# Hybrid encoder block on one core: norm weights spread by GpSimd, gate columns packed, setup reordered on three engines

## What is computed

```python
def rmsnorm(x, w):
    y = x * lax.rsqrt(jnp.mean(x * x, axis=-1, keepdims=True) + EPS)
    return y * w

h = rmsnorm(x, norm_w)
proj = h @ w_in          # 1024 x 6168: DeltaNet q, k, v, z and the 8-wide beta and alpha,
                         # attention q, k, v, z and the 8-wide forget logits, two merge gates
y_a = gated_deltanet(...)            # chunks of 64 tokens, 8 heads
y_b = forgetting_attention(...)      # softmax with a decay from the forget logits
x = x + (g_a * (y_a @ P_A) + g_b * (y_b @ P_B)) @ W_out
out = rmsnorm(x, final_norm_w)
```

## Time and profile before

| | |
|---|---|
| median of 3 runs | 949.03 us (947.95 to 949.48) |
| span of the profiled execution | 945.6 us |
| TensorE busy | 925.3 us (98%) |
| VectorE, ScalarE, GpSimd busy | 65%, 50%, 2% |
| DMA, mean | 111 GB/s |

### The profile page before, as it was taken

The page is one execution under the profiler, slowest core; times in us unless marked ns, Lnnn a source line. Parts: engine busy times, 40 slices in busy tenths (PEclk is TensorE's granted clock), DMA queues, the critical chain, the costliest instruction groups (busy, mean ns, idle before and its releaser), DMA issues.

```text
span 945.6 us, 15912 instructions
## 1 busy us (share of the span) xinstructions
PE 925.3 (98%) x6380; PEld 700.9 (74%) x6380; DVE 610.6 (65%) x982; ACT 471.8 (50%) x842; POOL 19.7 (2%) x28
## 2 busy tenths in 40 slices
PE   5999999999999999999999999999999999999997
PEld 4778787888888876676766666666667888888885
DVE  7487568799999934454496786767862433246252
ACT  7555654532866625532756547556554442334131
POOL 1000002020000000000000000000000000000000
PEclk9999999999999999999999999999999999999999
DMA  8111351249323393322553325234125323123162
GB/s 251 45 49 45 96 178 48 68 143 228 100 90 104 107 271 89 102 74 91 139 181 94 109 101 168 102 102 123 35 68 178 108 71 94 51 112 112 45 192 75
DMA packets 115744, 104.87 MB, mean 111 GB/s; under 512 B 34192, under 2 KB 95760, under 8 KB 115288
## 3 DMA queue, kind: packets, MB, share of 16 engines
q1 hardware_dynamic: 104008, 80.27, 30.6%
q10 hardware_dynamic: 10512, 19.40, 5.6%
q0 software_dynamic: 1152, 4.19, 1.3%
HBM read 76.84 MB, written 27.00 MB: 110 GB/s over the span
## 4 chain that ended last, share of the span: by engine, by line
PE 45%; DVE 3%; ACT 1%; DMA 1%; issue 1%; SPq 0%; DVEq 0%; ACTq 0%
PE pj L2182 6%; PE pj L2184 5%; PE pj L2183 5%; PE pc L2315 4%; PE pa L2281 3%; PE pa L2250 1%; PE pj L2193 1%; PE pj L2195 1%; PE pj L2194 1%; PE pb L2341 1%; PE pb L2330 1%; PE pc L2450 1%; PE pc L2449 1%; PE pb L2450 1%; PE pb L2449 1%; PE pa L2450 1%
## 5 line engine op out<-in xcount | busy, mean ns | idle before, releaser
L144 PE MATMUL pj<-h_hi,w_hi 128*128 128x512 f32 x504 | 203.6, 404 | 0.5 <-DVE w_lo L132 0.5
L145 PE MATMUL pj<-h_lo,w_hi 128*128 128x512 f32 x504 | 196.9, 391 | 0.0
L146 PE MATMUL pj<-h_hi,w_lo 128*128 128x512 f32 x504 | 196.5, 390 | 0.0
L144 PEld LDWEIGHTS pj<-h_hi,w_hi 128*128 128x128 f32 x504 | 94.5, 187 | 23.9 <-issue 1.1
L146 PEld LDWEIGHTS pj<-h_hi,w_lo 128*128 128x128 f32 x504 | 94.6, 188 | 20.4
L145 PEld LDWEIGHTS pj<-h_lo,w_hi 128*128 128x128 f32 x504 | 94.7, 188 | 18.0 <-issue 0.2
L2182 PE MATMUL pj<-h_hi,w_hi 128*128 128x512 f32 x248 | 101.2, 408 | 0.3 <-PEq L315 0.3
L2184 PE MATMUL pj<-h_hi,w_lo 128*128 128x512 f32 x248 | 96.8, 390 | 0.0
L2183 PE MATMUL pj<-h_lo,w_hi 128*128 128x512 f32 x248 | 96.7, 390 | 0.0
L2182 PEld LDWEIGHTS pj<-h_hi,w_hi 128*128 128x128 f32 x248 | 46.5, 188 | 19.6 <-issue 10.1
L572 ACT ACTIVATE xc<-pj 128x512 f32<-128x512 f32 x39 | 23.3, 597 | 72.4 <-PE pj L146 71.8
(11 more groups left out here) (366 smaller groups left out, 1858.2 us busy)
## 6 DMA issues: line engine op xcount, KB each, us to landing
w_raw<-in_w_in SPq DMA_DIRECT2D x48, 512.0 KB, 4.4
fox_scratch<-xc ACTq DMA_DIRECT2D x39, 256.0 KB, 2.7
qkv<-in_x SPq DMA_DIRECT2D x8, 512.0 KB, 6.8
fa<-rows_scratch POOLq DMA_DIRECT2D x8, 512.0 KB, 4.8
rv<-fr_scratch SPq DMA_DIRECT2D x16, 256.0 KB, 4.0
ma<-m_scratch SPq DMA_DIRECT2D x8, 512.0 KB, 4.4
rv<-in_w_out SPq DMA_DIRECT2D x8, 512.0 KB, 3.7
w_raw<-in_x SPq DMA_DIRECT2D x8, 512.0 KB, 4.5
```

What stands on the lines that cost most here:

```text
L144: nc.tensor.matmul(o, w_hi[:, slot, k], h_hi[:, k, cols], start=(k == 0), stop=False)
L145: nc.tensor.matmul(o, w_hi[:, slot, k], h_lo[:, k, cols], start=False, stop=False)
L146: last = nc.tensor.matmul(o, w_lo[:, slot, k], h_hi[:, k, cols], start=False, stop=(k == KT - 1))
```

## The change

- The norm weights are loaded as one row of 1024 (4 KB) into partition 0 of `att`, and GpSimd spreads it over the 128 partitions of `nw_bc` (`partition_broadcast`). VectorE waits for that (`nw_spread`).
- The gate columns are loaded side by side, 24 columns: beta and alpha are neighbours in w_in and come in one DMA, forget in another. `spread_rows` puts them at columns 0, 32 and 64 of w_hi and w_lo as they are split; the gaps there are zeroed by GpSimd, behind the spread. `w_raw` isn't zeroed any more.
- `stats` is taken apart into `square` and `root`; `SQUARED` and `ROOTED` hold the count of `rstd_step` after each. `high` and `low` are now called by half. All three orders are new.
- The products stay the same ones. Those of tokens 0 to 255 now begin after turn 2, turn 3 follows three k of them, and turns 4 to 7 all lie in tile 1.

```diff
--- before.py
+++ after.py
...
@@ -187,6 +189,7 @@
         masks = sem("masks")
         x_loaded = [sem(f"x_loaded{t}") for t in range(NT)]
         nw_loaded = sem("nw_loaded")
+        nw_spread = sem("nw_spread")
         rstd_step = sem("rstd_step")
         xs_done = sem("xs_done")
         x_turned = sem("x_turned")
@@ -252,7 +255,8 @@
 
...
-        TURNS = ((0, 1), (0, 5), (1, 1), (1, 5))
+        SQUARED = (1, 4, 7, 10, 13, 14, 19, 22)
+        ROOTED = (3, 6, 9, 12, 16, 18, 21, 24)
         ROWS = 2 * 32 + H
...
+        packed_rows = w_raw[:, 0, :, 0:3 * H].rearrange("p k (g c) -> p k g c", c=H)
+
+        def spread_rows(w):
+
+            return w[:, 0, :, 0:96].rearrange("p k (g c) -> p k g c", c=32)[:, :, :, 0:H]
+
         def spill_row(n):
 
             return (N_FOX + n - N_Z if n < N_F else n - N_F) * P
@@ -318,10 +328,8 @@
                 for t in range(4):
                     sp.dma_start(xt[:, t], x[0, P * t:P * t + P, :]).then_inc(x_loaded[t], 16)
 
-                sp.wait_ge(zeroed, 1)
-                sp.dma_start(w_raw[:, 0, :, 0:H], w_view[:, :, COL_B:COL_B + H]).then_inc(w_loaded[0], 16)
-                sp.dma_start(w_raw[:, 0, :, 32:32 + H], w_view[:, :, COL_A:COL_A + H]).then_inc(w_loaded[0], 16)
-                sp.dma_start(w_raw[:, 0, :, 64:64 + H], w_view[:, :, COL_F:COL_F + H]).then_inc(w_loaded[0], 16)
+                sp.dma_start(w_raw[:, 0, :, 0:2 * H], w_view[:, :, COL_B:COL_B + 2 * H]).then_inc(w_loaded[0], 16)
+                sp.dma_start(w_raw[:, 0, :, 2 * H:3 * H], w_view[:, :, COL_F:COL_F + H]).then_inc(w_loaded[0], 16)
                 load_w(sp, 1, tile_col(1), 1)
...
-                sp.wait_ge(zeroed, 2)
+                sp.wait_ge(zeroed, 1)
...
@@ -459,11 +467,14 @@
                     ins.then_inc(masks, 1)
                     pool.wait_ge(masks, made[0])
 
-                nc.gpsimd.memset(w_raw[:, 0], 0.0).then_inc(zeroed, 1)
                 nc.gpsimd.memset(rows_in[:, :], 0.0).then_inc(zeroed, 1)
                 link(nc.gpsimd.memset(ident[:, :], 0.0))
                 link(nc.gpsimd.affine_select(ident[:, :], ident[:, :], pattern=[[-1, P]], base=0,
                                              channel_multiplier=1, compare_op=ALU.not_equal, fill=1.0))
+                pool.wait_ge(nw_loaded, 16)
+                nc.gpsimd.partition_broadcast(nw_bc, nw_row).then_inc(nw_spread, 1)
+                nc.gpsimd.memset(w_hi[:, 0, :, 0:ROWS].bitcast(F32), 0.0).then_inc(zeroed, 1)
+                nc.gpsimd.memset(w_lo[:, 0, :, 0:ROWS].bitcast(F32), 0.0).then_inc(zeroed, 1)
...
-                act.dma_start(nw_bc, norm_w[0, :].partition_broadcast(P)).then_inc(nw_loaded, 16)
+                act.dma_start(nw_row, norm_w[0:1, :]).then_inc(nw_loaded, 16)
 
                 act.wait_ge(vec_step, 2)
 
-                def stats(t):
+                def square(t):
                     act.wait_ge(x_loaded[t], 16)
                     if t:
-                        act.wait_ge(rstd_step, 3 * t)
+                        act.wait_ge(rstd_step, SQUARED[t - 1])
                     nc.scalar.activation(tmp[:, :], xt[:, t], ACT.Square, accum_out=stat[:, t:t + 1]).then_inc(rstd_step, 1)
-                    act.wait_ge(rstd_step, 3 * t + 1)
+
+                def root(t):
+                    act.wait_ge(rstd_step, SQUARED[t])
                     nc.scalar.activation(stat[:, t:t + 1], stat[:, t:t + 1], ACT.Ln, bias=eps_t,
                                          scale=1.0 / D).then_inc(rstd_step, 1)
-                    act.wait_ge(rstd_step, 3 * t + 2)
+                    act.wait_ge(rstd_step, ROOTED[t] - 1)
                     nc.scalar.activation(stat[:, t:t + 1], stat[:, t:t + 1], ACT.Exp, scale=-0.5).then_inc(rstd_step, 1)
 
-                def high(t):
-                    for b in range(2):
-                        act.wait_ge(x_turned, 2 * t + b + 1)
-                        nc.scalar.activation(h_hi[:, 4 * b:4 * b + 4, P * t:P * t + P],
-                                             turn_banks[t % 2][:, b].rearrange("p (k c) -> p k c", c=P), ACT.Copy).then_inc(h_hi_done, 1)
-
-                stats(0)
-                stats(1)
-                stats(2)
-                high(0)
-                stats(3)
-                high(1)
+                def high(t, b):
+                    act.wait_ge(x_turned, 2 * t + b + 1)
+                    nc.scalar.activation(h_hi[:, 4 * b:4 * b + 4, P * t:P * t + P],
+                                         turn_banks[t % 2][:, b].rearrange("p (k c) -> p k c", c=P), ACT.Copy).then_inc(h_hi_done, 1)
+
+                square(0)
+                root(0)
+                square(1)
+                root(1)
+                square(2)
+                high(0, 0)
+                root(2)
+                high(0, 1)
+                high(1, 0)
+                high(1, 1)
+                square(3)
                 act.wait_ge(w_loaded[0], loads_of(0, 0))
-                nc.scalar.activation(w_hi[:, 0, :, 0:ROWS], w_raw[:, 0, :, 0:ROWS], ACT.Copy).then_inc(w_hi_done, 1)
-                high(2)
-                high(3)
-                stats(4)
+                act.wait_ge(zeroed, 2)
+                nc.scalar.activation(spread_rows(w_hi), packed_rows, ACT.Copy).then_inc(w_hi_done, 1)
+                root(3)
+                high(2, 0)
+                high(2, 1)
                 split_hi(act, 1, 0, 1)
-                for t in range(4, NT):
-                    if t + 1 < NT:
-                        stats(t + 1)
-                    high(t)
+                high(3, 0)
+                high(3, 1)
+                square(4)
+                square(5)
+                root(4)
+                root(5)
+                square(6)
+                high(4, 0)
+                root(6)
+                square(7)
+                high(4, 1)
+                root(7)
+                for t in range(5, NT):
+                    high(t, 0)
+                    high(t, 1)
...
-                dve.wait_ge(nw_loaded, 16)
+                dve.wait_ge(nw_spread, 1)
 
                 def scaled(t):
-                    dve.wait_ge(rstd_step, 3 * t + 3)
+                    dve.wait_ge(rstd_step, ROOTED[t])
                     if t >= 4:
                         dve.wait_ge(x_turned, 2 * (t - 4) + 2)
                     nc.vector.scalar_tensor_tensor(xs[:, t % 4], xt[:, t], stat[:, t:t + 1], nw_bc,
                                                    ALU.mult, ALU.mult).then_inc(xs_done, 1)
 
-                def low(t):
-                    for b in range(2):
-                        cols = slice(P * t, P * t + P)
-                        dve.wait_ge(h_hi_done, 2 * t + b + 1)
-                        nc.vector.tensor_tensor(h_lo[:, 4 * b:4 * b + 4, cols],
-                                                turn_banks[t % 2][:, b].rearrange("p (k c) -> p k c", c=P),
-                                                h_hi[:, 4 * b:4 * b + 4, cols].bitcast(F32), ALU.subtract).then_inc(h_done, 1)
+                def low(t, b):
+                    cols = slice(P * t, P * t + P)
+                    dve.wait_ge(h_hi_done, 2 * t + b + 1)
+                    nc.vector.tensor_tensor(h_lo[:, 4 * b:4 * b + 4, cols],
+                                            turn_banks[t % 2][:, b].rearrange("p (k c) -> p k c", c=P),
+                                            h_hi[:, 4 * b:4 * b + 4, cols].bitcast(F32), ALU.subtract).then_inc(h_done, 1)
 
                 scaled(0)
                 scaled(1)
+                low(0, 0)
                 scaled(2)
-                low(0)
+                low(0, 1)
+                low(1, 0)
+                low(1, 1)
+                dve.wait_ge(w_hi_done, 1)
+                dve.wait_ge(zeroed, 3)
+                nc.vector.tensor_tensor(spread_rows(w_lo), packed_rows, spread_rows(w_hi).bitcast(F32),
+                                        ALU.subtract).then_inc(w_ready, 1)
                 scaled(3)
-                low(1)
-                dve.wait_ge(w_hi_done, 1)
-                nc.vector.tensor_tensor(w_lo[:, 0, :, 0:ROWS], w_raw[:, 0, :, 0:ROWS], w_hi[:, 0, :, 0:ROWS].bitcast(F32),
-                                        ALU.subtract).then_inc(w_ready, 1)
-                low(2)
-                low(3)
+                for t in (2, 3):
+                    low(t, 0)
+                    low(t, 1)
+                split_lo(dve, 1, 1)
                 scaled(4)
-                split_lo(dve, 1, 1)
-                for t in range(4, NT):
-                    if t + 1 < NT:
-                        scaled(t + 1)
-                    low(t)
+                scaled(5)
+                low(4, 0)
+                scaled(6)
+                low(4, 1)
+                scaled(7)
+                for t in range(5, NT):
+                    low(t, 0)
+                    low(t, 1)
...
@@ -998,42 +1034,59 @@
                                                        xs[:, t % 4, (4 * b + k) * P:(4 * b + k + 1) * P], ident[:, :])
```

(81 more changed lines are left out.)

## The result

The kernel after takes 961.37 us (median of 5 runs, 961.25 to 966.93) against 949.03 (5 runs): ratio 1.0146, 95% interval 1.0129 to 1.0163. It is slower, as forecast, but by 12.3 us where 3.5 were forecast, and outside the range, which ended at 957.5.

A forecast was written before the change was run, and what follows sets the result against it. TensorE was taken as the bound, busy 925.3 of 945.6 us. The 945.6 us span, 3.5 for the later second half and 3.4 around the span gave 952.5 us; range 946.9 to 957.5.

The forecast's parts named there:

- The quantity to forecast: Shift of TensorE's first product of the second half of the tokens, at 32.52 us in the kernel before.
- one for one: Claim that any shift of the second half's start at 32.52 us reaches the kernel's end in full.
- Part 2: When GpSimd's spread weights are ready: one fetch of 8.0 us, as gate loads took, after the row; ready at 11.75.
- rival (D): GpSimd fetches its first set of operations again at the end, behind every other engine: 960.5 us; chance 0.06.
- main case: One fetch ahead of GpSimd's spread: S at 11.75, second half at 35.95, 952.5 us; chance 0.47.
- S: Start of VectorE's first scaling of x, 7.81 us in the kernel before; forecast 11.75.
- Part 1: Start: without the broadcast's packets x tile 0 lands at 5.0 instead of 5.95, giving S 6.8 if the spread is quick.
- rival (A): GpSimd's spread is quick: second half at 31.0, 1.5 us earlier, 947.5 us; chance 0.25.
- Part 3: New order, first scaling to second half: products from S+7.4, then waits at VectorE; S+24.2 against S+24.7, gain 0.5 us.
- Part 4: Gate columns in two loads, earlier later loads, GpSimd's zeroing memsets: all in time, costing nothing while their cover lasts.
- How the numbers follow: Sum to the run time: 3.4 us lie around the profiled 945.6 us span, and the same is added to the forecast.

The follow-up runs named there:

- e1: Kernel after with GpSimd's spread of the norm weights moved ahead of the memset and select that make the identity; 945.14 us against 948.89, ratio 0.9964.
- e3: Kernel before plus one GpSimd spread of 128 columns that nobody reads, right behind the first select; 952.65 us against 948.89, ratio 1.0041.
- e7: Kernel before with norm weights loaded as one row and spread by GpSimd ahead of its first select, order and gate columns untouched; 947.89 us, ratio 0.9993.
- e5: Kernel after plus a GpSimd addition behind the last selects of the first stage; 952.64 us against 948.62, ratio 1.0040.
- e4: Kernel after with norm weights brought by the kernel before's broadcast DMA, without GpSimd's spread: new order and packed gate columns alone; 947.61 us, ratio 0.9988.
- e6: Kernel before with the new order of norm steps, turns and first products alone, gate columns in three loads; 948.45 us, ratio 1.0003.

## Why the prediction was right or wrong

**The quantity to forecast** held: the loss lies ahead of the second half's start. It isn't carried to the microsecond: after has +13.54 at the start and +12.3 in the median, e1 -2.35 and -3.7. Single executions of the kernel before lie between 947.0 and 950.5, and a trace is one of them, so such differences are what one trace against a median can show. The traces show how far the shift is carried: at GpSimd's last select, 457.64 us in the kernel before, the kernel after is 13.51 later, e3 4.05 later and e1 2.29 earlier, nearly as at the second half's start. But e7, which was 1.43 ahead, is 0.37 later there, and e5 is 5.07 later where it was 3.95 later. Behind that point e4's trace takes 65.0 us from GpSimd's DMA issue near 505 to the one near 568, where the kernel before takes 61.4; the granted clock from 505 to 570 us is 0.97 in e4 and 1.00 in the kernel before. So "one for one" holds to 1.4 us in the medians, and a single execution can lose some us more. What e7 and e5 lose ahead of 457 us stays open.

**Part 2, the number of gaps, is the step that failed.** The text says "nothing in this trace is an operation of GpSimd that moves data between partitions" and prices one fetch ahead of the spread, while it keeps the select where it is: "the select that ended at 2.51 ends at about 1.6". It ended at 11.8. The 0.24 us ahead of the select was read as the price of a second kind of operation, but it holds only for a kernel without the new operation, or with the new one placed otherwise: 10.42 us stand ahead of the select in the kernel after and 11.30 in e3, 0.16 in e1 and 0.50 in e5. A second fetch was thought of, in rival (D), as one "at the end, behind every other engine" with 960.5 us; the sum was near, but the place was wrong. The kernel after has no gap at its end: behind its last select, at 471.15 us, GpSimd issues its next DMA after 0.18 us. The second gap stands at the start, ahead of the identity.

**Part 2, the size of one gap,** was 8.0 us from the gate loads. Measured ahead of the spread: 9.49 (after), 9.16 (e3) and 9.50 us (e5); ahead of the select: 10.42 (after) and 11.30 us (e3); ahead of the addition: 7.01 us at 205 us (e5). That it is a fetch over the DMA engines, behind the x tiles like the gate loads, was my supposition and isn't shown. The main case with one gap was S = 11.75, second half 35.95, 952.5 us. e5, which has exactly one gap at the start, measures 12.71, 36.47 and 952.64. The sum was near for a kernel that pays once; the kernel after pays twice. That the time is hit so closely is in part luck, as misses cancel. The fetch was put behind the landing of the row, from 2.8 on, but in e5 the gap begins at 1.88, right behind the select. It isn't made longer by the row: it takes 9.50 us there and 9.49 us in the kernel after, where it begins at 11.79, long after the row's two packets went through queue q10 (before 2.0 us). It is 1.5 us longer than the 8.0; the spread itself took 1.30 us (0.95 used). Together S is 0.96 later than forecast, and the stretch from S to the second half is 0.44 shorter.

Whether busy DMA engines make a gap longer isn't shown. For those ahead of the select and the addition it looks so: 10.42 and 11.30 us while the DMA engines are 88% and 91% busy, 7.01 us at 23%. For those ahead of the spread it doesn't: 9.49, 9.16 and 9.50 us at 56%, 66% and 98%. No run changed the traffic alone.

**Part 1** was right in sign and small in size. Tile 0 is squared at 4.38 (after) and 4.58 (e1); forecast 5.0 with bounds 4.1 and 5.95. With all gaps gone, S is 6.41 in e1 (forecast 6.8), as rival (A) says.

**Part 3** forecast S + 7.4 for the first product and S + 24.2 for the second half. Measured 7.28 and 23.45 in after, 7.54 and 23.76 in e1. The 24.2 was to be the effect of the order, "a gain of 0.5"; the order gives 0.38. The size was near, but the reason ("most of it waits again, at VectorE") isn't what the traces show. In e1 VectorE's last low half does end last, at 30.12, as forecast, but only 0.08 us behind TensorE's own work, the turn of `rows_in`, which ends at 30.04:

```profile
29.77 0.27 PE L1085 MATMUL pa<-ident,rows_in 128*128 128x128 f32 x1
...
28.84 1.28 DVE L787 TENSOR_TENSOR h_lo<-pb,h_hi 128x512 fp32r<-128x512 f32 x2
```

From the first product to the second half TensorE is as full as in the kernel before: 16.07 of 16.22 us in e1, 15.22 of 15.31 before. With the order alone (e6) the first product starts at S + 8.25 instead of S + 9.40, 1.15 us earlier, and the stretch behind it is 16.08 instead of 15.31, 0.77 us longer. That is turn 3, which has moved from ahead of the products to among them (0.8 by the forecast's own spacing). The difference is the 0.38.

**Part 4** held packing for free and without gain. Its loads were in time, but the smaller copies (0.35 us on each engine instead of 0.68 and 0.75) lie on the chain through ScalarE and VectorE to the first product, which starts at S + 7.50 in e4 and at S + 8.25 in e6; 0.60 of it is left at the second half.

**Rival (A)** is e1's case: forecast second half 31.0 and 947.5 us, measured 30.17 and 945.14. It decided by the order of two instructions, not by the kind of operation.

**How the numbers follow:** "3.4 lie around the span" is wrong. In each run whose span is known the time is 1.7 to 1.9 us longer than that run's own span. The rest was the distance of one quick execution (945.6 + 1.8 = 947.4) from the median. It did no harm, as it went into both sides.

## What to carry to other kernels

Ask of a new kind of operation on GpSimd not only what it costs but what it does to its neighbours, over the whole execution and into the next one, and try it ahead of the others: with the spread ahead of the first select no gap was left (e1, e7). A gap marked "issue" on GpSimd with no semaphore behind it, 7.01 to 11.30 us here, is the sign in the trace. When a change has several parts, each worth under 1.5 us, run the one with the new mechanism alone and read its trace before the times, since e1 and the kernel after differ by the place of one instruction and by 16.2 us.

## What the runs showed that was not expected

- What stands ahead of GpSimd's first select changes with what comes later in the program: 10.42 us in the kernel after, 0.50 us with an addition at 212 us (e5). What the execution before left behind would explain it. An unread spread of 0.43 us in e3 delays an earlier instruction by 11.30 us. e1's 945.14 us holds for executions that follow one another; what its first execution after another kernel takes wasn't measured.
- The gap ahead of the first select took 10.42 and 11.30 us (after, e3), that ahead of the addition 7.01 us at 205 us (e5), and that ahead of the spread 9.16 to 9.50 us in three traces, with the DMA engines 56% to 98% busy.
- A norm row of 4 KB instead of a broadcast of 512 KB lets x tile 0 land 1.4 to 1.6 us earlier (squared at 4.38 in after, 4.54 in e7 and 4.58 in e1, against 5.99), and is worth 1.4 us at the second half's start even with the order of the kernel before (e7). In e7's time that isn't clear of noise. With the new order and packing the medians of e1 and e4, which differ in how the norm weights come, are 2.5 us apart (945.14 and 947.61).
